# A hybrid attention, RWKV-7 and SwiGLU layer in split fp32: remainders moved from GpSimd to VectorE, seven places for normed planes, another order in the pairs' tails, and the last projection in two halves

## What is computed

```python
h = rmsnorm(x, norm1_g)
proj = h @ w_in                      # q, k, v | RWKV-7 features | 2 merge gates
att = swa_prompt(q, k, v, attn_sinks)          # window 128, chunks of 64
rw, S_new, shift_new = rwkv7_mix(p_rw, shift0, S0, ...)   # recurrent state 64x64 per head
u = einsum('btnc,ncd->btnd', stack([att, rw]), w_branch)
x = x + sum(sigmoid(gates) * u) @ w_out
h2 = rmsnorm(x, norm2_g)
x = x + (silu(h2 @ w_ffn_gate) * (h2 @ w_ffn_up)) @ w_ffn_down    # 2816 wide
y = rmsnorm(x, final_norm_g)
```

## Time and profile before

| | |
|---|---|
| median of three runs | 3268.34 us (3265.31 to 3269.6) |
| profiled execution | 3266.61 us, span 3264.8 us |
| mean granted TensorE clock | 0.994 |
| TensorE busy | 3174.8 us, 97% |
| VectorE / ScalarE / GpSimd busy | 1565.1 / 1019.3 / 473.5 us |
| transfers | 528.07 MB, mean 162 GB/s |

### The profile page before, as it was taken

How to read it: one execution, slowest core, us unless ns; L and a number is a source line. 1 busy time by engine, 2 the same in 40 slices (tenths; PEclk the granted TensorE clock), 3 DMA queues, 4 the chain that set the end, 5 groups by cost and what they waited for, 6 DMA issues and landing times.

```text
span 3264.8 us, 65637 instructions
## 1 busy us (share of the span) xinstructions
PE 3174.8 (97%) x27835; PEld 2667.1 (82%) x27835; DVE 1565.1 (48%) x2542; ACT 1019.3 (31%) x1848; POOL 473.5 (15%) x405
## 2 busy tenths in 40 slices
PE   8999999999999999999999999999999999999998
PEld 6777778777777878877777878998777789999997
DVE  6566544467666574444553156304555523432223
ACT  5444333344444343332321133302333312310001
POOL 1023110121112020021210012003212111000000
PEclk9999999999999999999999999999999999999999
DMA  4454442266666763544444673265343445465554
GB/s 156 151 190 156 149 155 95 92 220 208 198 210 211 246 212 95 162 160 134 136 138 143 193 225 123 91 203 171 122 126 124 132 152 171 140 204 174 175 176 148
DMA packets 265986, 528.07 MB, mean 162 GB/s; under 512 B 33632, under 2 KB 35296, under 8 KB 265696
## 3 DMA queue, kind: packets, MB, share of 16 engines
q1 hardware_dynamic: 265696, 523.88, 49.8%
HBM read 411.78 MB, written 112.08 MB: 160 GB/s over the span
## 4 chain that ended last, share of the span: by engine, by line
PE 89%; DVE 6%; issue 2%; ACT 1%; DMA 1%; POOL 1%; SPq 0%; DVEq 0%; ACTq 0%; POOLq 0%
PE PS L798 76%; PE PS L833 6%; PE PS L891 1%; PE PS L946 1%; DVE wl L1585 1%; DMA y<-xres 1%; DVE op L2036 1%; PE PS L1117 1%; PE PS L967 1%; PE PS L1131 0%; PE PS L881 0%; ACT L1146 0%; PE PS L1135 0%; PE PS L915 0%; PE PS L908 0%
## 5 line engine op out<-in xcount | busy, mean ns | idle before, releaser
L798 PE MATMUL PS<-hh,wh 128*128 128x512 f32 x1872 | 770.1, 411 | 2.1 <-issue 1.2
L798 PE MATMUL PS<-hh,wl 128*128 128x512 f32 x1872 | 732.6, 391 | 0.0
L798 PE MATMUL PS<-hl,wh 128*128 128x512 f32 x1872 | 731.5, 391 | 0.0
L1165 ACT ACTIVATE wh<-raw 128x512 fp32r<-128x512 f32 x452 | 283.8, 629 | 483.4 <-PE PS L798 376.0
L1585 DVE TENSOR_TENSOR wl<-raw,wh 128x512 fp32r<-128x512 f32 x452 | 332.7, 739 | 206.2 <-ACT wh L1165 201.0
L798 PEld LDWEIGHTS PS<-hh,wh 128*128 128x128 f32 x1872 | 352.1, 188 | 93.6 <-issue 16.3
L798 PEld LDWEIGHTS PS<-hh,wl 128*128 128x128 f32 x1872 | 352.2, 188 | 77.0
L798 PEld LDWEIGHTS PS<-hl,wh 128*128 128x128 f32 x1872 | 352.8, 188 | 74.2 <-issue 8.1
L798 PE MATMUL PS<-hh_last,wh 128*128 128x272 f32 x1280 | 266.0, 289 | 2.1 <-DVE xres L1678 2.1
L798 PE MATMUL PS<-hl_last,wh 128*128 128x272 f32 x1280 | 264.6, 288 | 0.0
L798 PE MATMUL PS<-hh_last,wl 128*128 128x272 f32 x1280 | 263.1, 287 | 0.0
(11 more groups left out here) (280 smaller groups left out, 4870.6 us busy)
## 6 DMA issues: line engine op xcount, KB each, us to landing
wh<-weight_hi SPq DMA_DIRECT2D x492, 256.0 KB, 2.8
wl<-weight_lo SPq DMA_DIRECT2D x492, 256.0 KB, 3.0
raw<-w SPq DMA_DIRECT2D x186, 512.0 KB, 3.6
weight_hi<-wh SPq DMA_DIRECT2D x164, 256.0 KB, 4.5
weight_lo<-wl SPq DMA_DIRECT2D x164, 256.0 KB, 4.7
raw<-w SPq DMA_DIRECT2D x76, 256.0 KB, 3.4
gate_scratch<-gst SPq DMA_DIRECT2D x48, 256.0 KB, 3.6
gb<-gate_scratch SPq DMA_DIRECT2D x24, 512.0 KB, 5.3
```

The source lines that it names most:

```text
L798: mm = pe.matmul(PS[:, bank(t) + f, 0:t.cols], wt[:, cols], mov[:, m, f * t.cols:f * t.cols + t.cols], start=(first and a == 0), stop=(n = ...
L1165: act.activation(wh[h % 4][:], src, ACT.Copy).then_inc(hi_done, 1)
```

## The change

1. The remainders ml, fl and hl (176 instructions) move from GpSimd's list to VectorE's, with the same tags. GpSimd keeps the elementwise steps of the pairs.
2. The ring of normed planes of norm2 has seven places: e1, acc, accn and four planes of xin. Seven scaled planes carry earlier tags. In exchange gst has four planes instead of eight.
3. NRAW goes from 6 to 7, and the first norm's sum, Ln, Exp and planes get later tags.
4. In the last chunk of a pair, oo is computed before the update of st.
5. The last group of the last down projection is made in two passes of 272 columns (stages Fd0 and Fd1), each followed by its own squares, sum, Ln, Exp, scaling and store; its weights are loaded for each pass. ScalarE's table for Ln is loaded after the last fh.

```diff
-NRAW = 6
+NRAW = 7
...
+            if b == NB - 1 and s == len(GROUPS) - 1:
+                for f in range(2):
+                    self.down(b, s, f)
...
-            gst = place("gst", [128, KD, MT], at_r4)
+            gst = place("gst", [128, 4, MT], at_r4)
...
+        ring = [t[:] for t in (e1, acc, accn)] + [xin[:, 4 + i, :] for i in range(4)]
...
-                return {"rawhi": -87.5 + 0.8 * k, "rawlo": -86.3 + 0.8 * k, "sq": -20 + 2 * k, "add": -19 + 2 * k, "ms": 9.0,
-                        "ln": 10.0, "ex": 11.0, "t": 14 + 3 * k, "hi": 15 + 3 * k, "lo": 16 + 3 * k}[part]
+                return {"rawhi": -87.5 + 0.8 * k, "rawlo": -86.3 + 0.8 * k, "sq": -20 + 2 * k, "add": -19 + 2 * k, "ms": 17.1,
+                        "ln": 18.0, "ex": 19.0, "t": 21 + 3 * k, "hi": 22 + 3 * k, "lo": 23 + 3 * k}[part]
...
-                return z + {"t": -17.4 + 2 * k if k >= 3 else -20.5 + 1.3 * k, "hi": -13.7 + 2 * k, "lo": -12.4 + 2 * k}[part]
+                return z + {"t": -26.0 + 1.3 * k if k < 7 else -11.9, "hi": -13.7 + 2 * k, "lo": -12.4 + 2 * k}[part]
...
                         act.activation(fh[b][:, k, 0:T], acc[:, 0:T], ACT.Copy).then_inc(f_hi, 1)
+                        if b == NB - 1 and j == NFF - 1:
+                            log_table()
...
-            run(leads(), merged(), ffn(), norm1(), norm2(), fronts(), tails())
+            run(leads(), fronts(), tails())
...
+            def ffn_rest():
+                for b in range(NB):
+                    T = width(b)
+                    for j in range(NFF):
+                        yield tile("Fu", b, j).last + (4.6 if b == NB - 1 else 3.5)
+                        dve.wait_ge(f_hi, b * NFF + j + 1)
+                        k = j - sum(g for i, g in enumerate(GROUPS) if sum(GROUPS[:i + 1]) <= j)
+                        dve.tensor_tensor(fl[b][:, k, 0:T], acc[:, 0:T], fh[b][:, k, 0:T], ALU.subtract).then_inc(f_lo, 1)
...
+            def norm2_rest():
+                for m, (what, b) in enumerate(SUMS):
+                    T = width(b)
+                    for k in range(KD) if what[0] != "F" else ():
+                        yield n2_tag(m, k, "lo")
+                        dve.wait_ge(h_hi, KD * (N1 if what == "X" else N2)[b] + k + 1)
+                        dve.tensor_tensor(hl[b][:, k, 0:T], ring[k % 7][:, 0:T], hh[b][:, k, 0:T], ALU.subtract).then_inc(h_lo, 1)
...
+                    for what in (output, state) if c == pr.chs[-1] else (state, output):
+                        what(c)
...
-            run(rest(), raw_first(), projections(), merged(), output(), ffn(), norm1(), norm2(), fronts(), tails())
+            run(rest(), raw_first(), projections(), merged(), output(), ffn(), norm1(), norm2(range(len(SUMS) - 1)), norm2((len(SUMS) - 1,)), merged_rest(), ffn_rest(), norm1_rest(), norm2_rest(), fronts(), tails())
```

More of the change, by code:

```diff
@@ L187, in ffn, with down @@
                         self.column(*c)
-            if not (open_end and s == len(GROUPS) - 1):
+            if b == NB - 1 and s == len(GROUPS) - 1:
+                for f in range(2):
+                    self.down(b, s, f)
+            elif not (open_end and s == len(GROUPS) - 1):
                 self.down(b, s)
-    def down(self, b, s):
+    def down(self, b, s, half=None):
         g = GROUPS[s]
+        stage = "Fd" if half is None else f"Fd{half}"
         per = KD // g
         for first in range(0, KD, per):
-            tiles = [self.tile("Fd", b, s * KD + first + d) for d in range(per)]
+            tiles = [self.tile(stage, b, s * KD + first + d) for d in range(per)]
+            if half is not None:
+                for t in tiles:
+                    t.h, t.half = 1, half
             source = [(group_unit(s) + 2 * g + first + d, g, 0) for d in range(per)]
@@ L600, in n2_tag @@
                 z = Q["F", b]
-                return z + {"t": -17.4 + 2 * k if k >= 3 else -20.5 + 1.3 * k, "hi": -13.7 + 2 * k, "lo": -12.4 + 2 * k}[part]
-            t = tile("Fd", b, (len(GROUPS) - 1) * KD + k)
+                return z + {"t": -26.0 + 1.3 * k if k < 7 else -11.9, "hi": -13.7 + 2 * k, "lo": -12.4 + 2 * k}[part]
             if part in ("sq", "add"):
-                return t.last + {"sq": 2.2, "add": 3.5}[part]
-            end = tile("Fd", b, len(GROUPS) * KD - 1).last
+                return final(what, b, k).last + {"sq": 2.2, "add": 3.5}[part]
+            end = final(what, b, KD - 1).last
             return end + {"ms": 4.9, "ln": 6.2, "ex": 7.4, "t": 10.0 + 3 * k}[part]
@@ L696, in y_out @@
             def y_out():
-                for b in range(NB):
+                for b in range(NB - 1):
                     for k in range(KD):
@@ L702, in y_out @@
                             sp.dma_start(y[:, k, there], xres[b][:, k, own]).then_inc(y_st[k], 16)
+                first = CH + (NB - 1) * BT
+                for f, cols in enumerate((((0, HT, first),), ((HT, BT, first + HT), (BT, MT, 0)))):
+                    for k in range(KD):
+                        yield n2_tag(len(SUMS) - 2 + f, k, "t") + 1.0
+                        sp.wait_ge(y_done, (NB - 1 + f) * KD + k + 1)
+                        for a, z, there in cols:
+                            sp.dma_start(y[:, k, there:there + z - a], xlast[:, k, a:z]).then_inc(y_st[k], 16)
             def small():
@@ L1170, in shifted @@
                         t = tile("A", b, i)
-                        yield t.last + 1.05
+                        yield max(t.last + 1.05, 20.5 + 1.4 * i) if b == 0 and i < NRAW else t.last + 1.05
                         act.wait_ge(dense, t.last + 1)
@@ L1282, in norm1, with norm2 @@
                         act.activation(hh[bb][:, k, 0:T], nt[k % 2][:, 0:T], ACT.Copy).then_inc(h_hi, 1)
-            def norm2():
-                sq, ring = [acc, e1], [e1, acc, accn]
-                for m, (what, b) in enumerate(SUMS):
-                    T = width(b)
+            def norm2(which):
+                sq = [acc, e1]
+                for m in which:
+                    what, b = SUMS[m]
+                    own = share(what, b)
                     for k in range(KD):
@@ L1713, in ffn @@
                         j += 1
[L1714 to L1720 removed]
+                        for f in ("0", "1") if b == NB - 1 and s == len(GROUPS) - 1 else ("",):
+                            for d in range(KD):
+                                t = tile("Fd" + f, b, s * KD + d)
+                                yield t.last + 1.05
+                                dve.wait_ge(dense, t.last + 1)
+                                if s:
+                                    dve.wait_ge(*freed(tile("Fd", b, s * KD + d - KD)))
+                                residual(t, b, d)
             def scaled_pair(b, j, T):
@@ L2038, in tail, with state, output @@
                 b0_, b1_ = 6, 7
+                def state(c):
+                    dve.wait_ge(T2, pr.at("T2", f"ds{c}"))
+                    tt_(f"st1{c}", st[:], st[:], q8(b1_), ALU.add)
+                    own(f"st1{c}")
+                    pcv = pcol[:, 0:4 * n].rearrange("p (a c) -> p a c", c=n)[:, :, c:c + 1].to_broadcast([128, 4, CH])
+                    tt_(f"st2{c}", st[:], st[:], pcv, ALU.mult)
+                def output(c):
+                    dve.wait_ge(T2, pr.at("T2", f"o2{c}"))
+                    for par, name in enumerate(("E", "O")):
+                        r, there = half_rows(par), half_rows(1 - par)
+                        tt_(f"o{name}{c}", v4(oo)[r, :, CH * c:CH * c + CH], v4(op)[there, :, CH * c:CH * c + CH],
+                            q8(b0_, there), ALU.add)
                 for c in pr.chs:
```

157 lines of the change are left out of this document (71 added, 86 removed).

## The result

The changed kernel takes 3245.34 us (median of 4 runs, 3243.59 to 3246.72) against 3267.09 us before, a ratio of 0.9934 (95% interval 0.9922 to 0.9945): 0.66% faster, where I had forecast 3245. The profiled execution has a span of 3244.7 us, 20.1 less than before. The forecast was met as a sum, and that is luck in part: one of its terms had the wrong sign and others made up for it. The experiments found a version that is another 8 us faster.

A forecast was written before the change was run, and what follows sets the result against it. TensorE, busy 3174.8 of 3264.8 us, was taken as the bound, leaving its waits and low-clock time to win. Terms summed to -22.0 from 3266.6, giving 3244.6; the forecast was 3245, range 3234 to 3259.

The forecast's parts named there:

- wait at 1463, with clock: TensorE's 5.87 us wait for sv shrinks to 1.6, saving 4.3, and 3.1 of low clock is regained: -7.4 us.
- wait at 290, with clock: TensorE's 3.98 us wait for sv gets 0.9 shorter, with part of the low clock regained: -2.0 us together.
- wait at 650: TensorE's wait for kvp goes whole as VectorE's steps ahead of it shorten: -3.3 us; it could be 0.
- fl: Remainder of 0.69 instead of 1.32 us comes earlier, cutting TensorE's two waits and low clock at 684 to 692: -3.2 us.
- start: The first norm's sum moves eight products back, which fill TensorE's 3.5 us wait for nsum: -3.5 us.
- output ahead of state: TensorE's five waits for oo behind two st, 6.4 us, each lose up to 0.84: -3.7 us.
- the end: Behind TensorE's last product, halves and an earlier table load save 4.1; extra sum +0.7, doubled weight loads +0.5: -2.9 us.
- new waits: VectorE waits for ScalarE's copy before a remainder, delaying what stands behind; 4 hits at 1.0: +4.0 us.
- Rival 3: Loads bound the last projection, 7.4 MB taking 21 us instead of 18: +3, so 3248 us; chance 0.2.
- rivals 1, 2 and 5: VectorE's in-order waits decide, 3275 and above (0.04); relief taken back, 3259 (0.2); nothing seen, 3262 to 3275 (0.06).
- rival 4: More is won: short waits go too and the clock stays up at 290: -9, so 3236 us; chance 0.15.

The follow-up runs named there:

- a_start_old: Changed kernel with the start of before (six raw tiles, first norm's sum after eight quanta, old plane tags): 3249.55 us.
- a_swap: Changed kernel with the last projection's two passes in the other order, columns 272 to 543 first: 3242.24 us.
- a_whole: Changed kernel with its last down projection and final norm whole again, ScalarE's table still loaded ahead: 3240.89 us.
- a_last_two: Changed kernel with only the last two units of the last down projection in two passes, columns 272 to 543 first, sample columns in one store: 3238.97 us.
- a_fronts_dve: Changed kernel with the remaining elementwise steps of the pairs' fronts also moved from GpSimd to VectorE: 3253.28 us.
- a_dummy: Changed kernel with eight small unneeded subtractions of 48 columns on GpSimd in place of each moved remainder: 3301.97 us.
- a_rest_pool: Changed kernel with all 176 remainders back on GpSimd, everything else as changed: 3251.47 us.
- a_whole_9st: Changed kernel with last projection and final norm whole, table load ahead, and 9 stores at the end instead of 16: 3238.77 us.
- b_rest_ring: Kernel before with both the remainders on VectorE and the ring of seven places: 3251.98 us.

## Why the prediction was right, and where it was wrong

By its own steps, against the lead between two points of the table above:

| step | predicted | lead gained |
|---|---|---|
| wait at 1463, with clock | -7.4 | -5.7 (1455 to 1476) |
| wait at 290, with clock | -2.0 | -2.9 (283 to 302) |
| wait at 650 | -3.3 | -3.5 (648 to 670) |
| fl | -3.2 | -3.2 (2.5 from 670 to 690, 0.7 near 2877) |
| start | -3.5 | -2.5 (to 60); 2.9 by a_start_old's span |
| output ahead of state | -3.7 | -3.9 (near 218, 371, 781 and 2427), less a new wait of 0.9 at 1456 that is in the first row |
| the end | -2.9 | +1.9 (21.9 at 2900, 20.1 at the end) |
| new waits | +4.0 | +2.0 (before 648, near 1185 and 1960) |

The rest of the way holds 2.3 us more, small waits each under 1 us. The row of 290 is not steady: where the program is the same, the changed kernel and a_swap gain 2.9 there, a_whole, a_last_two and a_start_old 4.4.

**The mechanism held**, at the large waits. Scaled planes take 746 where I had said near 800; for sv I had said under 8 together and none over 3.2, and it is 8.4 and 2.2; there is no low clock at 1463. Over the whole kernel before, 33 scaled planes of 512 columns overlap an operation of GpSimd by over 0.2 us and take 1421 ns, 39 are alone and take 744. a_fronts_dve shows the contention by itself, 903 against 686 on the same instructions. The rule of the Trainium skill (GPSIMD Engine Reference, § 8, Key points) that a VectorE instruction with two SBUF inputs contends with GpSimd agrees with it: xres, with one operand in PSUM, stayed at 688. What is not shown is how much of the 7.4 us of the move is the contention and how much the shorter remainder (0.69 for 1.32): a_dummy was to tell, and did not.

**That the wait at 1463 came out at 1.43 where I had said 1.6 is luck in part.** I had counted five remainders behind pp; one of them stands ahead of it, 0.7 less. I had added 1.0 each for zz and kk; in fact zz, kk and cc stretch three remainders, to 1.77, 1.37 and 1.53, 2.6 together. I had also taken the company of the rows of before wrongly: the plane of 1.78 at 1460.09 runs beside zz (1459.57, 1.75 long) and mxs beside kk (1462.99, 1.27 long), not beside a remainder, and the remainders there take 1.27 to 2.09 and not 1.75 each. So part of the stretching came from steps that the change leaves on GpSimd. GpSimd's row, before:

```profile
1459.57 1.75 POOL L1525 TENSOR_TENSOR zz__103<-cc__106,zz__103 128x512 f32<-128x512 f32 x1
```

**What I had too narrow** is the share of the ring. I gave nearly the whole gain to the remainders' move; ring alone gives 9.1 us and remainders alone 7.4. The ring takes four scaled planes out of the stretch before sv, which stood there with 0.74 alone and 1.65 to 1.78 in company, whoever makes the remainders. That a late GpSimd is felt through ScalarE's list too, as in a_rest_pool, I had not seen.

**The step that failed is the end**, with "1112 to 1124 shows 354: it just fits, +0.5". Two passes take TensorE 6.4 us more in the projection, where I had counted 1.2, and it waits there for wl, 3.1 us in all; that it waits for wh was one of the signs of being wrong that I had named. A rate that the core reached in one window of 12 us was taken for one that a chain of loads with four places keeps up; there such windows moved 213 to 314 GB/s. The Trainium skill's figure (DMA: Bandwidth & Descriptors, Specifications) is some 358 GB/s for a core; the highest windows of 12 us that I find here are 360 before and 366 after, both from 6 to 18 us, so the trace is at that figure or a little above it. So the core reaches that rate elsewhere; here the loads had to wait for places too. How much of the 3.1 us is the rate and how much the second pass's order of tiles stays open. Rival 3 (+3 us for loads) was the nearest and still too small. What I had won behind the projection was also not all the halves': of 4.3 us to the first store 2.3 come with the table load and the sum, and stay without the halves.

My rivals 1, 2 and 5 did not happen; TensorE waits for a moved remainder 3.0 us in all (fl and fl_last). Of rival 4 the short waits went in part, 2.3 us, but the clock at 290 did not stay up.

## What to carry to other kernels

Where one engine's list is full of two-SBUF-operand work, look at what runs beside it before looking at its own instructions: 176 remainders of 129 us together raised its busy time by 60, because its other work got shorter. Moving all of such work is not better: what stands in one dependent chain may be faster on two lists that disturb each other. Before loading something twice, compare the needed rate with what the loads reach with these few places, not with the best window, and look when each place comes free; and count the instructions that issue the stores at the end, since here 16 of them took 7.6 us beside 3.4 us of scaling.

## What the hardware showed that I had not expected

A store costs SyncE's queue 0.33 us of issue behind a pause and 0.43 to 0.46 right behind another, of 120 KB or of 16 KB alike: giving the eight small ones to one instruction of 0.59 us took 1.3 us off the end.

TensorE's granted clock after equal waits was not the same from profile to profile. Thirteen profiles have the same wait of 3.0 us for sm, near 145 us. Over the 5 us behind it the granted clock was 1.00 in four of them (before, after, a_whole_9st, b_rest_ring) and between 0.50 and 0.73 in the other nine; at 0.66 those 5 us hold 1.7 us less of full clock. So a part of every term that contains the clock, some 2 us a place, is not the change's.
